# The rotation's two transfers moved to SyncE's queue, with three smaller moves and 21 added matmuls, in a two-block model on one core

## What is computed

```python
h = rms_norm_2(x, norm_pre);  proj = h @ w_in          # q, k, v, z, ... of five branches, and the gates
y_sb = flat(stick_breaking(heads(sb_q), heads(sb_k), heads(sb_v)))
h_ml = mlstm(heads(q_ml), heads(k_ml), heads(ml_v), ml_i + b_igate, ml_f + b_fgate)
y_ml = flat(head_norm(h_ml)) * jax.nn.sigmoid(ml_o)    # head_norm subtracts the mean of each head
y_gm = spatial_gating(jax.nn.gelu(gm_u), jax.nn.gelu(gm_v), gm_ln_g, gm_ln_b, gm_ws, gm_bs)
y_rt = flat(head_norm(retention(rotary(heads(rt_q), positions), rotary(heads(rt_k), positions), heads(rt_v))))
y_xa = flat(memory_attention(heads(xa_q), mem_k, mem_v))
ys = jnp.stack([y_sb * silu(sb_z), y_ml * silu(ml_z), y_gm * silu(gm_z), y_rt * silu(rt_z), y_xa * silu(xa_z)], axis=2)
up = jnp.einsum('bsnw,nwd->bsnd', ys, w_up)
merged = jnp.sum(sigmoid(gates) * up, axis=2)
x = x + rms_norm_2(merged @ w_out, norm_post)
# rotary: t1, t2 = halves of a head; concatenate([t1*cos - t2*sin, t1*sin + t2*cos])
```

## Time and profile before

| | us |
|---|---|
| median of 3 timed runs | 2201.73 (2200.91 to 2202.25) |
| the profiled execution | 2199.61, of which span 2197.8 |
| TensorE busy, share of the span | 1866.3, 85% |
| VectorE busy | 1035.7, 47% |
| ScalarE busy | 407.9, 19% |
| mean granted TensorE clock | 0.942 |
| first block and experts | 0 to 1186 of the span |
| layer 0, layer 1 | 1189 to 1690, 1690 to 2198 |

### The profile page before, as it was taken

One profiled execution on the slowest core, in us unless ns is written; L12 is line 12 of the kernel. 1 busy time (PEld: TensorE's weight loads), 2 busy tenths in 40 slices (PEclk: granted clock), 3 DMA queues, 4 the chain that ended last, 5 costly groups with the idle time before them and its releaser, 6 DMA issues. The chain is left out here.

```text
span 2197.8 us, 27405 instructions
## 1 busy us (share of the span) xinstructions
PE 1866.3 (85%) x11528; PEld 1162.8 (53%) x11528; DVE 1035.7 (47%) x1612; ACT 407.9 (19%) x787; POOL 0.2 (0%) x4
## 2 busy tenths in 40 slices
PE   8999977758666667766667999989999999989998
PEld 5687733323323333322223897874446898874445
DVE  7858522212112122122222768678663557768662
ACT  1123300000000000000001233223323233223322
POOL 0000000000000000000000000000000000000000
PEclk9999998888988888888998999999999999999999
DMA  7222899999999999999998334454533334454430
GB/s 307 81 77 102 342 434 429 431 430 432 430 431 429 433 430 430 431 429 430 430 433 348 144 130 159 142 222 153 188 121 136 143 127 169 134 194 193 160 147 19
DMA packets 32375, 595.02 MB, mean 271 GB/s; under 512 B 3966, under 2 KB 5248, under 8 KB 7560
## 3 DMA queue, kind: packets, MB, share of 16 engines
q1 hardware_dynamic: 30344, 584.31, 64.7%
q10 hardware_dynamic: 1920, 9.09, 1.3%
HBM read 590.22 MB, written 1.06 MB: 269 GB/s over the span
## 5 line engine op out<-in xcount | busy, mean ns | idle before, releaser
L2289 PE MATMUL ps<-ring,arena 128*32 128x512 f32 x2032 | 285.9, 714 | 156.3 <-DMA ring<-in_w_experts 147.6
L897 PE MATMUL ps<-ring,arena 128*128 128x512 f32 x656 | 286.4, 592 | 0.0
L2289 PEld LDWEIGHTS ps<-ring,arena 128*32 128x32 f32 x2032 | 72.0, 128 | 354.6 <-issue 219.3
L897 PEld LDWEIGHTS ps<-ring,arena 128*128 128x128 f32 x656 | 124.3, 190 | 155.0 <-issue 155.0
L2323 PE MATMUL ps<-ring,arena 128*32 128x256 f32 x2016 | 151.2, 450 | 62.8 <-DMA ring<-in_w_experts 62.1
L713 PE MATMUL ps<-arena,ring 128*128 128x128 f32 x1536 | 183.2, 275 | 2.7 <-issue 1.8
L713 PEld LDWEIGHTS ps<-arena,ring 128*128 128x128 f32 x1536 | 177.3, 192 | 5.4 <-issue 4.0
L2953 DVE COPY arena<-ps 128x256 f32<-128x256 f32 x64 | 27.2, 425 | 273.0 <-PE ps L2323 273.0
L713 PE MATMUL ps<-early,ring 128*128 128x128 f32 x1152 | 137.3, 275 | 2.9 <-DVE ring L1557 2.9
L2323 PEld LDWEIGHTS ps<-ring,arena 128*32 128x32 f32 x2016 | 70.5, 126 | 130.0 <-issue 76.6
L713 PEld LDWEIGHTS ps<-early,ring 128*128 128x128 f32 x1152 | 133.3, 192 | 4.5 <-DVE ring L1557 3.3
(11 more groups left out here) (476 smaller groups left out, 2471.8 us busy)
## 6 DMA issues: line engine op xcount, KB each, us to landing
ring<-in_w_experts SPq DMA_DIRECT2D x88, 4096.0 KB, 23.4
ring<-in_w_layers SPq DMA_DIRECT2D x64, 2048.0 KB, 7.8
ring<-in_w_experts SPq DMA_DIRECT2D x13, 2048.0 KB, 13.4
ring<-in_w_first SPq DMA_DIRECT2D x9, 2048.0 KB, 8.3
early<-in_w_layers SPq DMA_DIRECT2D x6, 2048.0 KB, 7.9
arena<-in_w_mem SPq DMA_DIRECT2D x4, 2048.0 KB, 20.1
ring<-in_w_first SPq DMA_DIRECT2D x4, 512.0 KB, 7.3
early<-in_w_experts SPq DMA_DIRECT2D x1, 2048.0 KB, 25.2
```

Source lines behind the costliest of these rows:

```text
L897: last = pe.matmul(ps[:, bank, :], lhs[:, k, :], rhs[:, k, :], start=(first and k == 0), stop=(k == n - 1), skip_group_check=True)
L2289: last = pe.matmul(ps[CAP * e:CAP * (e + 1), v // 4, :], xg[:, (v % 4) * 2 + k, CAP * e:CAP * (e + 1)], w[:, k, e, :], start=(v % 4 == 0 a ...
```

## The change

It moves four pieces of code and adds matmuls whose results nobody reads. In the lists of before and after, line numbers differ by up to 16, since lines were added.

```diff
@@ layers_sync
                     if i >= RING2:
                         unit_end(i - RING2)
+                        if UNITS[i] == "gm_u":
+                            whole(sp, l, "rt_k")
+                            for half in range(2):
+                                sp.dma_start(xr(rt_turned)[64 * half:64 * half + 64, :], rt_qk[64 - 64 * half:128 - 64 * half, :]).then_inc(sem("in_turned"), 16)
@@ layers_pe
+        def hold_clock(pe, bank, n):
+            for _ in range(n):
+                pe.matmul(ps[:, bank, 0:P], ones, ones, start=True, stop=True)
...
+                hold_clock(pe, 7, 13 if l else 2)
                 unit_in(plan.unit_at["gm_v"])
...
                 evacuated(pe, job("sb_v", 1))
-                w("gm_mix", 4, 4)
                 for hd in range(NH):
                     run(2)
                     w("sb_sp", NH, hd + 1)
+                    if hd == 0:
+                        w("gm_mix", 4, 4)
@@ layers_act
                 run(1)
-                whole(act, l, "rt_k")
-                for half in range(2):
-                    act.dma_start(xr(rt_turned)[64 * half:64 * half + 64, :], rt_qk[64 - 64 * half:128 - 64 * half, :]).then_inc(sem("in_turned"), 16)
                 run(2)
@@ layers_dve
                 dve.tensor_scalar(wide_flat, wide_flat, 1e18, None, ALU.min).then_inc(sem("ml_qkm"), 1)
+                centre_values("ml_v", ml_v, ml_sum, "ml_vc")
                 run(3)
...
                 gate_bound("ml_o")
-                centre_values("ml_v", ml_v, ml_sum, "ml_vc")
                 run(2)
@@ the merge, layers_dve
+                def second_sums(b):
+                    add_product(b, 1, g22, G_BANK[2], "gate_prod", "gate_c", "gate_q")
+                    add_product(b, 1, u22, U_BANK[2], "up_prod", "up_c", "up_q")
+                    bound(b, 1, g22)
...
+                    if b == 0:
+                        second_sums(b)
                     if b + 1 < NBR:
                         gate_difference(b + 1)
                         gate_total(b + 1)
                         up_sums(b + 1)
-                    add_product(b, 1, g22, G_BANK[2], "gate_prod", "gate_c", "gate_q")
-                    bound(b, 1, g22)
-                    add_product(b, 1, u22, U_BANK[2], "up_prod", "up_c", "up_q")
+                    if b:
+                        second_sums(b)
@@ after the last expert, tensor
             expert_group(pe.snap(more_rounds * NGRP + NGRP - 1), tail=True)
+            hold_clock(pe, 0, 6)
```

More of the change, by code:

```diff
@@ L1539, in layers_dve, with centre_values @@
                     dve.tensor_tensor(y, y, ps[:, 5, 0:SEQ], ALU.mult).then_inc(sem("xa_y"), 1)
+                def centre_values(name, v, sums, done):
+                    for m in range(2):
+                        evacuated(dve, job(name, m))
+                        heads = v[:, m, :].rearrange("p (h n) -> p h n", h=NH)
+                        link(dve.tensor_reduce(sums[:, m, :], heads, AX, ALU.add))
+                        dve.scalar_tensor_tensor(heads, sums[:, m, :].unsqueeze(2).to_broadcast([P, NH, HD]), -1.0 / HD, heads, ALU.mult, ALU.add).then_inc(sem(done), 1)
                 run(2)
@@ L1549, in layers_dve @@
                 gate_bound("ml_o")
-                def centre_values(name, v, sums, done):
-                    for m in range(2):
-                        evacuated(dve, job(name, m))
-                        heads = v[:, m, :].rearrange("p (h n) -> p h n", h=NH)
-                        link(dve.tensor_reduce(sums[:, m, :], heads, AX, ALU.add))
-                        dve.scalar_tensor_tensor(heads, sums[:, m, :].unsqueeze(2).to_broadcast([P, NH, HD]), -1.0 / HD, heads, ALU.mult, ALU.add).then_inc(sem(done), 1)
-                centre_values("ml_v", ml_v, ml_sum, "ml_vc")
                 run(2)
```

## The result

| | before | changed |
|---|---|---|
| median of the timed runs, us | 2201.32 (4 runs, 2200.91 to 2202.25) | 2170.42 (4 runs, 2167.61 to 2171.63) |
| the profiled execution, us | 2199.61, span 2197.8 | 2171.63, span 2169.9 |
| mean granted TensorE clock | 0.942 | 0.945 |

A forecast was written before the change was run, and what follows sets the result against it. TensorE was taken to bound both layers. Gains of 15.8 + 6.1 + 2.9 + 1.8 + 1.6 = 28.2 us, less 0.7, take 2199.6 to 2172.1 us; 2.1 us from profile to median gives 2174.2 us, range 2170.5 to 2184.

The forecast's parts named there:

- The rotation: Transfers ahead of VectorE's rotated products, both layers: issued by SyncE before the gm_u load, TensorE's waits and slow clock go, 15.8 us.
- the mechanism that was named: In SyncE's one queue the two transfers are served ahead of the gm_u load instead of sharing the DMA engines with it.
- The landing: The two transfers arrive 6.5 us after first issue: 4.4 us for the bytes, about 1 us on either side.
- 1.6 us in hand: Layer 0 margin between transfers landing and the limit, 8.1 us after issue, where TensorE's wait is gone; about 1 us in layer 1.
- Two signs of the prediction: Expected in the new profile: VectorE idle under 1 us before its first rotation line; the two transfers landing in 6 to 8 us.
- The second sums: Merge, branch 0: sums moved ahead of preparing branch 1 remove TensorE's 2.17 us wait per layer and 1.73 us slow clock, 6.1 us.
- third rival: Clock fell behind 2.17 us idle in layer 0 only, so may not hold at the start: 2176 us; chance 0.18 with small new waits.
- VectorE becomes the bound: Rival: VectorE late by 2 us before branch 1 and at the rotation, both layers, 8 to 10 us lost: 2183 us, chance 0.12.
- The values and the mix: mLSTM values centred in VectorE's idle time, ending near 1360, 2.9 us; gm mix wait moved behind two products, 1.8 us.
- The added matmuls: Six behind the experts and two after the barrier hold layer 0's starting clock, 1.6 us; thirteen before layer 1 gain nothing.
- the clock falls all the same: Rival at the start of layer 0: the clock isn't sure to hold, 2 us less gained, 2176 us; chance 0.18 with small new waits.
- given back: 0.7 us taken off the summed gain for small waits appearing when TensorE runs closer to the other engines.

## Why the prediction was right, and where it was wrong

**The rotation: right, by the mechanism that was named.** The forecast 15.8 us against 16.1 us (rotation back on ScalarE, start left out), 15.0 us (load first) and 15.7 us (rotation alone: 16.9, less 1.7 at the merge, and 0.5 for a start that was slower by that), each from one profile. The landing was sized too short: 6.5 us forecast from the first issue, 6.8 us measured in layer 1 and 7.0 and 8.25 us in layer 0. The load behind it in the queue is not to blame, since held back it leaves 6.8 and 7.9 us; what is short is the 2.1 us that I set beside the 4.4 us of the bytes, and no run takes that apart. (The 12.7 us that the prediction sets against the 6.5 us are a median counted from each transfer's own issue; from the first issue before had 13.9 and 13.1 us.) Of the "1.6 us in hand" between 1.1 us and nothing were left. In seven profiles with the rotation ahead of the unit in SyncE's queue and not split by tensor, layer 0 has 8.2 us in five, with a wait of about 0.6 us on TensorE, and 7.0 and 7.3 us in two, without; what makes the difference is open. Two signs of the prediction failed with it: VectorE's idle time under 1 us, and a landing within 8 us, both in layer 0.

**The second sums: the size differs from profile to profile.** Forecast 2.17 + 2.17 + 1.73 us; with the sums back it was 8.1 us in one profile. The term takes for granted that the clock behind such a wait falls in layer 0 and holds in layer 1, though the prediction itself says under its third rival that this differs. Over six profiles with the old order, it fell in 4 of 12 places, in either layer. The feared new waits on VectorE ("VectorE becomes the bound") never appeared.

**The values and the mix: right in kind, 4.7 us forecast, 5.7 us measured.** VectorE has the values centred at 1358.8 us; the forecast 1360 did not count that the work runs 1.1 us earlier there, since the mix's wait is gone ahead of it.

**The added matmuls: the start right, the 13 wrong.** "In a gap of 3.1 us in front of layer 1, where the clock stayed at 1.00 without them: nothing gained." That was one execution. Without the 13 the gap took 17.61 us in 2 of 7 profiles and 19.31 to 20.67 us in 5; with them it took 17.61 us in all 7. At the start all 6 profiles without the added matmuls have 20.1 to 21.5 us, and of 8 with them 7 have 18.73 us and one 20.43 us: the rival "the clock falls all the same" is real and came once in eight.

**Each wait was undersized.** A matmul's listed end is modelled, and the idle time is counted from it. From start to start, the rotation's wait in layer 0 is 5.97 us (1443.86, less the 1437.89 us at which the 32 rows ahead of it end when their first start and their rate are taken), not 5.80; the merge's 2.33 us, not 2.17; those of the values and the mix 0.25 us more each. Over eight waits this is 1.6 us, and with 0.4 us of a ninth small wait that went too (line 750 in layer 0, 1432.93 us) it explains the 2 us by which the layer part beat the sum. The 0.7 us "given back" were 0.9 us in one profile and nothing in the other.

**The sum, then.** Two steps failed. One is pricing a wait at the idle time that the profile lists for it. The other is reading each slow clock, and its absence, from one execution as its fixed price, above all in the "nothing gained" for the thirteen matmuls. By the mean of three profiles of before and two of the changed kernel the gains are 2.3 us (start), 13.6, 1.8 (gap) and 13.0 us, 30.7 us in all, which is the 30.5 us between the medians of 51 and 8 executions. The forecast had 1.6, 14.9, 0 and 11.7 us less 0.7, 27.5 us in all. The 3.2 us between them split as follows, when the matmuls of each profile of before are set beside the same ones of the changed kernel's second profile. The waits were 2.1 us longer than counted (1.0 us of it at the values and the mix). The slow clocks come to 0.9 us more: 1.8 too little in the gap, 0.7 at the start and 0.4 in layer 1, against 1.9 too much in layer 0, whose first profile had both slow clocks at their worst. The rest, 0.2 us, is what was given back for nothing. So the largest single term that was off, the 0 for the thirteen matmuls, was hidden by too dear a layer 0, and that was luck. The range's low end, "the whole sum without the 0.7 us, and a better distance", allowed only 3.7 us for all of this. That the step from profile to median (2.1 us) isn't a constant shows as well: the second and third profiles of before lie 0.7 us under and 2.9 us above the 2200.6 us.

## What to carry to other kernels

When two transfers share the engines and one of them is waited for, put that one ahead in one queue, or hold the other back: here the order was worth 15 us, the issuing engine nothing. Read what a wait costs from start to start, and take the slow clock behind it as a chance with a price, from several profiles, since the same wait may cost 2.3 or 4.0 us and one at full clock in the profile may be slow in most executions. Compare profiles by stage, with the untouched stages apart, before you call a forecast confirmed.

## What the hardware showed that was not expected

- Behind one and the same wait of TensorE the granted clock holds in some profiles and falls in others (14 profiles of 11 kernels, on at least three chips): behind 2.17 us (the merge) it fell in 4 of 12 cases, behind 3.10 us (ahead of layer 1) in 5 of 7, behind 3.79 us (start) in 6 of 6. Behind the 5.2 to 5.8 us wait of the rotation it fell in all 10 cases, at prices from 1.5 to 3.0 us: from line 755 to the wait of 0.46 us of line 713 it is 23.3 to 24.75 us, against 21.77 us without the wait.
- Thirteen matmuls with no use, in a gap in which TensorE had nothing to do, went with a full clock behind it in 7 of 7 profiles (17.61 us); without them the gap took the same 17.61 us in 2 of 7 and 1.7 to 3.1 us more in 5. Taken out alone they cost 1.7 us, in one profile. Six and two around the barrier went with a full clock in 7 of 8, where it fell in 6 of 6 without.
- A transfer of 1.05 MB within the on-chip memory in two parts is there for VectorE 6.8 and 7.9 us after the first issue when alone, 6.8 to 8.2 us with a unit of 2.10 MB behind it in its queue, 13.1 to 13.9 us with the unit in another queue and 12.8 and 13.2 us behind the unit.
